# A second block run as one program, with its gated linear unit between two halves of the attention branch

## The reference, cut to what matters

```
attn = sliding_window_attention(q, k, v, sinks)                  # 256 x 1024
y_val, y_gate = split(gelu(s5_ssm(u)) @ w_glu + b_glu)           # 512 -> 2 x 512
ssm = y_val * sigmoid(y_gate)                                    # 256 x 512
merged = sigmoid(gate_attn) * (attn @ w_branch_attn)             # 1024 -> 2048
       + sigmoid(gate_ssm) * (ssm @ w_branch_ssm)                # 512 -> 2048
x = x + merged @ w_out
h = rms_norm(x)
val, gate = split(h @ w_up)                                      # 2048 -> 2 x 5632
x = x + (val * gelu(causal_conv(gate))) @ w_down
out = rms_norm(x)
```

## Time and profile before

| | us |
|---|---|
| median of 3 runs | 3060.67 (3060.24 to 3062.17) |
| the profiled execution's own time | 3060.64 |
| span of its trace | 3058.8 |
| PE busy in it | 2850.6 (93%) |
| PE weight loads | 2793.8 (91%) |
| DVE busy | 1841.8 (60%) |
| ACT busy | 1234.2 (40%) |
| POOL busy | 513.3 (17%) |
| granted PE clock, mean | 0.968 of full |

### The profile page before, as it was taken

One profiled execution on the slowest core, in us unless ns is written; L12 is line 12 of the kernel. 1 busy time (PEld: TensorE's weight loads), 2 busy tenths in 40 slices (PEclk: granted clock), 3 DMA queues, 4 the chain that ended last, 5 costly groups with the idle time before them and its releaser, 6 DMA issues. The chain is left out here.

```text
span 3058.8 us, 60793 instructions
## 1 busy us (share of the span) xinstructions
PE 2850.6 (93%) x24170; PEld 2793.8 (91%) x24170; DVE 1841.8 (60%) x2106; ACT 1234.2 (40%) x1472; POOL 513.3 (17%) x586
## 2 busy tenths in 40 slices
PE   7998687799998999999999969999889999999997
PEld 7998585689997999999999969999889999999997
DVE  7657744556443565554555566698556655765665
ACT  4344112353332544343434434533345443444343
POOL 1000120337000325810191120000121010010011
PEclk9999788899999999999999989999999999999999
DMA  6553000354651656575656635555455565565554
GB/s 228 193 193 108 14 1 1 138 177 153 210 190 55 209 188 194 195 235 193 192 193 193 234 110 184 203 173 173 142 169 184 200 193 193 192 196 194 192 190 145
DMA packets 138262, 513.89 MB, mean 168 GB/s; under 512 B 15344, under 2 KB 15600, under 8 KB 136816
## 3 DMA queue, kind: packets, MB, share of 16 engines
q1 hardware_dynamic: 138096, 511.58, 50.7%
HBM read 503.12 MB, written 8.40 MB: 167 GB/s over the span
## 5 line engine op out<-in xcount | busy, mean ns | idle before, releaser
L638 PE MATMUL acc<-a,hi 128*128 128x256 f32 x3136 | 873.4, 279 | 41.3 <-DVE lo L465 30.8
L639 PE MATMUL acc<-a,hi 128*128 128x256 f32 x3136 | 868.2, 277 | 0.0
L640 PE MATMUL acc<-a,lo 128*128 128x256 f32 x3136 | 868.1, 277 | 0.0
L465 DVE TENSOR_TENSOR lo<-raw,hi 128x1024 fp32r<-128x1024 f32 x416 | 524.9, 1281 | 368.9 <-ACT hi L351 367.4
L638 PE MATMUL acc<-a,hi_f 128*128 128x256 f32 x2304 | 637.5, 277 | 11.7 <-DVE lo_f L465 11.0
L639 PE MATMUL acc<-a,hi_f 128*128 128x256 f32 x2304 | 637.1, 277 | 0.0
L640 PE MATMUL acc<-a,lo_f 128*128 128x256 f32 x2304 | 637.0, 276 | 0.0
L638 PEld LDWEIGHTS acc<-a,hi 128*128 128x128 f32 x3136 | 590.9, 188 | 46.1 <-issue 37.1
L639 PEld LDWEIGHTS acc<-a,hi 128*128 128x128 f32 x3136 | 591.0, 188 | 0.8 <-issue 0.5
L640 PEld LDWEIGHTS acc<-a,lo 128*128 128x128 f32 x3136 | 590.9, 188 | 0.0
L465 DVE TENSOR_TENSOR lo_f<-raw_f,hi_f 128x1024 fp32r<-128x1024 f32 x288 | 383.3, 1343 | 334.1 <-ACT hi_f L351 333.6
(11 more groups left out here) (509 smaller groups left out, 4277.7 us busy)
## 6 DMA issues: line engine op xcount, KB each, us to landing
raw_f<-in_ffn SPq DMA_DIRECT2D x256, 512.0 KB, 3.6
raw_in<-in_w_in SPq DMA_DIRECT2D x96, 512.0 KB, 3.5
raw<-in_w_in SPq DMA_DIRECT2D x92, 512.0 KB, 3.7
raw<-in_up_gate SPq DMA_DIRECT2D x88, 512.0 KB, 4.2
raw<-in_up_val SPq DMA_DIRECT2D x88, 512.0 KB, 4.3
raw<-in_down SPq DMA_DIRECT2D x88, 512.0 KB, 3.4
raw_x<-in_w_out SPq DMA_DIRECT2D x32, 512.0 KB, 4.2
raw_x<-in_wq SPq DMA_DIRECT2D x32, 512.0 KB, 3.3
```

What stands on the lines that cost most here:

```text
L465: eng.tensor_tensor(self.lo[:, slot, :], self.raw[:, slot, :], self.hi[:, slot, :].bitcast(F32), ALU.subtract).then_inc(self.s_lo, 1)
L638: eng.matmul(out, self.hi[:, slot, cols], a[:, 0, :], start=opens, stop=False)
L639: eng.matmul(out, self.hi[:, slot, cols], a[:, 1, :], start=False, stop=False)
L640: ins = eng.matmul(out, self.lo[:, slot, cols], a[:, 0, :], start=False, stop=closes)
```

## The change

- The two programs become one: the lists of phases are joined, the barriers and the clearing between them are gone, and so are `prefetch`, `ahead`, `split` and `skip`. The semaphores are allocated in the outer scope and given back in one list at the end of the feed-forward, ahead of the final norm.
- `br_attn` is cut in two halves of 4 units. The order becomes `br_attn` (first half), `glu_g`, `glu_v`, `br_attn` (second half), `br_ssm`, `w_out_2`.
- `glu_v` writes its result to tiles 4 to 7 of `a0`, no longer to `ah`, which the second half of `br_attn` still reads. `br_ssm` reads it there and writes to `a1`; `w_out_2` reads `a1` and writes `a0`; the `gate` and `val` phases read `a0`, `val` writes `a1` and `down` reads it. Before, these had `a0` and `a1` the other way round. `a1` keeps its place in memory, over the tables.
- `br_ssm` gets `lead`: in its unit v ACT makes the copy of chunk v+1 (in unit 0 those of chunks 0 and 1) ahead of the finish of unit v-1. Its loop is written out (`body` 8).

```diff
@@ def act
-                if not (ph is split and isinstance(v, int) and v == 0):
+                if ph.lead:
+                    for w in range(0 if v == 0 else v + 1, min(v + 2, ph.units)):
+                        self.act_split(eng, ph, w, w)
+                else:
                     self.act_split(eng, ph, v, j, first if first and v == 0 else None,
                                    first if first and v == 1 else None)
...
-        if ahead:
-            self.act_split(eng, ahead, 0, 0)
@@ def dve
-                for k in range(0 if ph is split and isinstance(v, int) and v == 0 else ph.nc):
+                for k in range(ph.nc):
...
-        for k in range(ahead.nc if ahead else 0):
-            self.split_low(eng, ahead, 0, 0, k)
@@ def second_block, into which gates_and_branches goes
+        sem = semaphores(nc, st)
+        with ExitStack() as early:
+            tab = alloc(nc, early, "s_tab", [P, 2, S5_COLS])
+            reals = alloc(nc, early, "s_xr", [P, 2, QT, T])
+            small = [alloc(nc, early, n, [P, 2, NH]) for n in ("mxs", "nmx", "smw", "skw")]
+            slp = alloc(nc, early, "slp", [P, NH])
         room = alloc(nc, st, "a1_room", [P, (LINE - 128) // 4])
         a1 = alloc(nc, st, "a1_3", [P, KT, 2, T], F32R)
...
-        ba = s.phase("br_attn", "br_attn", 8, 2, 2, ah, "br_attn", out=ub,
+        ba = s.phase("br_attn", "br_attn", 4, 2, 2, ah, "br_attn", out=ub,
                      ready=lambda eng: eng.wait_ge(window.low, 4))
         g1 = s.phase("glu_g", "glu", 2, 1, 4, s.a0, "glu_gate", out=gl, g="b_glu", g0=4,
                      ready=lambda eng: eng.wait_ge(space.low, 1))
-        g2 = s.phase("glu_v", "glu", 2, 1, 4, s.a0, "glu_val", out=ah, src=gl, w0=2)
-        bs = s.phase("br_ssm", "br_ssm", 8, 1, 4, ah, "br_ssm", out=s.a0, src=ub, g0=KT, after=g2)
-        phs = [ba, g1, g2, bs]
-        wo = s.phase("w_out_2", "w_out_2", 8, 4, 2, s.a0, "resid", g="ffn2_g", after=bs)
+        g2 = s.phase("glu_v", "glu", 2, 1, 4, s.a0, "glu_val", out=s.a0, t0=4, src=gl, w0=2)
+        bb = s.phase("br_attn", "br_attn", 4, 2, 2, ah, "br_attn", out=ub, t0=8, w0=8)
+        bs = s.phase("br_ssm", "br_ssm", 8, 1, 8, s.a0[:, 4:8], "br_ssm", out=a1, src=ub, g0=KT, after=g2, lead=True)
+        wo = s.phase("w_out_2", "w_out_2", 8, 4, 2, a1, "resid", out=s.a0, g="ffn2_g", after=bs)
+        phs = [ba, g1, g2, bb, bs, wo]
...
-                s.prefetch(eng, wo)
...
-                s.act(eng, phs, aside=space.act_last, at=ba, last=ps, ahead=wo)
+                s.act(eng, phs, aside=space.act_last, at=ba, last=ps)
...
-                s.dve(eng, phs, aside=space.dve_last, at=ba, last=ps, ahead=wo)
+                s.dve(eng, phs, aside=space.dve_last, at=ba, last=ps)
```

More of the change, by code:

```diff
@@ L140 @@
     ready: object = None
+    lead: bool = False
     base: object = None
@@ L308, in prefetch, with act @@
             self.load(eng, ph, c, c)
-    def act(self, eng, phs, aside=None, emit=None, at=None, last=None, ahead=None, split=None):
+    def act(self, eng, phs, aside=None, emit=None, at=None, last=None):
         at = at or phs[-1]
@@ L432, in act_finish, with dve @@
             ins.then_inc(done, 1)
-    def dve(self, eng, phs, aside=None, at=None, emit=None, last=None, finish=True, ahead=None, split=None):
+    def dve(self, eng, phs, aside=None, at=None, emit=None, last=None, finish=True):
         at = at or phs[-1]
@@ L1896, with __init__ @@
     BANKS = 4
-    def __init__(self, nc, s, ua, ah, pa, tab, keys, probs, stack):
+    def __init__(self, s, ua, ah, pa, tab, keys, probs, small, slp, sem):
         self.s, self.ua, self.ah, self.pa = s, ua, ah, pa
@@ L1904, in __init__ @@
         self.pt = probs.rearrange("p (a b) t -> p a (b t)", a=2)
-        self.mxs, self.nmx, self.sm, self.sk = (alloc(nc, stack, n, [P, 2, NH]) for n in ("mxs", "nmx", "smw", "skw"))
-        self.slp = alloc(nc, stack, "slp", [P, NH])
-        sem = semaphores(nc, stack)
+        self.mxs, self.nmx, self.sm, self.sk = small
+        self.slp = slp
         (self.zeroed, self.slopes, self.placed, self.vturned, self.vcopied, self.scored, self.biased, self.maxed,
@@ L2165, with __init__ @@
     EACH = 9
-    def __init__(self, nc, dram, s, ua, pa, gates, window, states, tab, xr, xi, bq, stack):
+    def __init__(self, dram, s, ua, pa, gates, window, states, tab, xr, xi, bq, sem):
         self.dram, self.s, self.ua, self.pa, self.gates, self.window = dram, s, ua, pa, gates, window
@@ L2355, in second_block @@
         clear_pads(nc, s)
-        wo = gates_and_branches(nc, dram, s, ub, ah, ua, states)
+        sem = semaphores(nc, st)
[4 more added lines that the diff above has]
+            slp = alloc(nc, early, "slp", [P, NH])
         room = alloc(nc, st, "a1_room", [P, (LINE - 128) // 4])
         a1 = alloc(nc, st, "a1_3", [P, KT, 2, T], F32R)
[L2359 to L2398, removed]
         xr = reals[:, 0], reals[:, 1]
@@ L2401, in gates_and_branches @@
         bq = ua[:, Q2 + QT:Q2 + 2 * QT, :].rearrange("p a t -> p (a t)"), s.th[:].rearrange("p a b t -> p (a b t)")
+        gl = ua[:, Q2:Q2 + 4, :]
         spare = ub[:, 0:2, :]
@@ L2409, in gates_and_branches @@
                      g0=GA2 + 2 * raw, w0=w0 + 4 * raw)
-        window = WindowAttention(nc, s, ua, ah, pa, tab, xr[0], ub[:, KT:2 * KT, :], st)
-        space = StateSpace(nc, dram, s, ua, pa, ps, window, states, tab, xr, xi, bq, st)
-        ba = s.phase("br_attn", "br_attn", 8, 2, 2, ah, "br_attn", out=ub,
+        window = WindowAttention(s, ua, ah, pa, tab, xr[0], ub[:, KT:2 * KT, :], small, slp, sem)
+        space = StateSpace(dram, s, ua, pa, ps, window, states, tab, xr, xi, bq, sem)
+        ba = s.phase("br_attn", "br_attn", 4, 2, 2, ah, "br_attn", out=ub,
                      ready=lambda eng: eng.wait_ge(window.low, 4))
@@ L2415, in gates_and_branches @@
                      ready=lambda eng: eng.wait_ge(space.low, 1))
-        g2 = s.phase("glu_v", "glu", 2, 1, 4, s.a0, "glu_val", out=ah, src=gl, w0=2)
-        bs = s.phase("br_ssm", "br_ssm", 8, 1, 4, ah, "br_ssm", out=s.a0, src=ub, g0=KT, after=g2)
-        phs = [ba, g1, g2, bs]
-        wo = s.phase("w_out_2", "w_out_2", 8, 4, 2, s.a0, "resid", g="ffn2_g", after=bs)
+        g2 = s.phase("glu_v", "glu", 2, 1, 4, s.a0, "glu_val", out=s.a0, t0=4, src=gl, w0=2)
[3 more added lines that the diff above has]
+        phs = [ba, g1, g2, bb, bs, wo]
+        for q, t0 in enumerate((0, KT, 2 * KT)):
+            n = min(KT, FT2 - t0)
+            gate = s.phase("gate", "up_gate", n // 2, 4, 2, s.a0, "gate", out=ub, g="c2", g0=3 * t0, p0=t0,
+                           taps=3, w0=2 * t0, after=wo if q == 0 else None, sum_after=q == 0)
+            val = s.phase("val", "up_val", n // 2, 4, 2, s.a0, "val", out=a1, src=ub, w0=2 * t0)
+            down = s.phase("down", "down", 8, n // 4, 4 if n % 16 else 2, a1, "sumsq" if q == 2 else "acc",
+                           w0=32 * q, after=val)
+            phs += [gate, val, down]
         with nc.Block() as block:
@@ L2480, in _ @@
                 s.pe(eng, phs)
-    return wo
+    final_norm(nc, s, "final2_g", out_dram)
 def build(nc, dram, out_dram):
```

## The result

The changed kernel takes 3038.9 us (median of 4 runs, 3032.3 to 3043.1), the one before 3061.4 in the same session (3060.2 to 3063.3): the ratio is 0.9924, with a 95% interval of 0.9911 to 0.9936. In a later session it was 3037.8 against 3062.1, ratio 0.9922 (0.9905 to 0.9938). So some 23 us are gone, 0.77%.

The account below looks back on a forecast made before the run. PE bounds the kernel, losing 32.3 us from glu_g to w_out_2's second chunk. With 8.1 lost after, 24.2 won less 0.8 for clearing gives 23.4 off 3060.64: 3037.2 us, range 3033.5 to 3041.

Parts of the forecast that it names:

- GLU after four units: glu_g starts 21.8 us earlier at no cost, its input being ready; the GLU's own losses of 1.48 + 1.03 stay.
- Second half of `br_attn`: Behind glu_v: the 3.99 us wait for POOL goes, 1.2 lost waiting for DVE's first subtraction; clock stays full.
- `br_ssm` with the lead: ACT's copy leaves the circle in br_ssm; 2.0 us lost there, bounds 0.3 to 3.5.
- the circle through DVE and POOL: In br_ssm, POOL waits for DVE's subtraction and L517 for POOL: 3.06 us a chunk.
- its chunks 2 to 7 start 2.9 to 3.1 apart: Sign to look for in PE's timeline of br_ssm: a pitch of 2.9 to 3.1 us.
- Rival (a): POOL and DVE don't meet: br_ssm loses 1.0 us, the step to w_out_2 1.8; 3035.6 us; chance 0.20.
- Step into `w_out_2`: From br_ssm: the lead ends, ACT copies w_out_2's first chunk behind unit 6's finish; 2.4 us lost, bounds 0.5 to 3.5.
- Clearing: Giving back the semaphores between feed-forward and final norm costs 0.8 us more, bounds 0.3 to 1.6.
- Swap of the buffers: a0 and a1 trade places in w_out_2 and feed-forward; matmuls take 0.1132 us from either, so 0 cost.
- Rival (b): PE's clock falls in br_attn's second half after three idle gaps; price 2.5 to 2.8 us, 3040 us; chance 0.08.
- (c): In br_ssm the lead frees nothing because ACT's early copy waits; pitch near 4.4, 12 us lost, 3047 us; chance 0.05.
- (d): Buffer swap slows w_out_2 and feed-forward, some 298 chunks; 0.1 us more each gives 3067 us; chance 0.02.

Follow-up runs that it names:

- two_ahead: lead_all, but in br_ssm ACT copies two chunks ahead of its finish and DVE subtracts one ahead of its evacuation; 3031.6 us, ratio 0.9899.
- lead_over: Changed kernel with ACT's lead carried over the phase border: w_out_2's first chunk copied ahead of the finish of br_ssm's unit 6; 3035.8 us, ratio 0.9920.
- no_clear: Changed kernel with the second block's semaphores held to the program's end, so no clearing ahead of the final norm; 3041.0 us, ratio 0.9937.
- lead_all: lead_over with the lead also in glu_g and glu_v and into the second half of br_attn; 3030.4 us, ratio 0.9904.
- both: Changed kernel with the edits of lead_all and no_clear together; 3031.8 us, ratio 0.9903.

## Why the prediction was right

The forecast was 3037.2, and two medians of the changed kernel are 3038.9 and 3037.8. Some of that nearness is luck: the four runs behind the first median reach from 3032.3 to 3043.1, beyond the forecast range on both sides, and the first block alone can move a run by more than most of the terms. By its own steps, in the profiled execution:

- *GLU after four units.* 0 was forecast for `glu_g`'s wait, and PE does not wait there. 1.48 + 1.03 was kept, and measured 1.48 + 1.03.
- *Second half of `br_attn`.* 1.2 was forecast, 1.20 at the gap and 0.11 in the next chunk were measured. The clock held there: the first chunk behind the gap took 2.80 to 2.83 in all executions with these three gaps.
- *`br_ssm` with the lead.* The term that was mis-sized: 2.0 was forecast, 0.9 measured. For the circle through DVE and POOL the prediction took "1.14 + 1.30 + 0.62 = 3.06 a chunk". In `two_ahead`, where DVE from 2196.36 on no longer waits for PE, this circle is 2.84. Of the 0.22 too much, 0.07 lies between the subtraction's start and POOL's end (2200.45 - 2198.08 = 2.37 for 2.44), and the rest behind POOL's end, where the next subtraction starts 0.46 and not 0.62 later. So the circle through PE, which stood beside it with 2.8 to 2.94, is the longer one, at 2.87; in the changed kernel L515 waits for PE, and POOL has all but ended when L517 comes. The sign "its chunks 2 to 7 start 2.9 to 3.1 apart" was met by three of the six steps only: they are 2.83 to 2.91. Rival (a), with 1.0 for `br_ssm`, had this number right but not its reason: POOL and DVE do meet, and it costs PE next to nothing there.
- *Step into `w_out_2`.* 2.4 forecast, 2.06 and 0.08 measured, and the fourth chunk did not wait. It was "ACT's finish and copy", as `lead_over` shows; PE's idle there was 1.78.
- *Clearing.* 0.8 forecast; 0.62 measured for itself, but with the clock it came to 1.4 in one execution and 0.7 in the other. The prediction had no term for the clock there.
- *Swap of the buffers.* 0 forecast, and 1767 matmuls per 200 us on both sides.

Lost: 6.9 for 8.1. Won there 25.4 for 24.2, less 1.5 at the end for 0.8, together 23.9 where 23.4 was forecast. The three errors, 1.1 and 0.3 in favour and 0.7 against, cancel in part. Rival (b), a fall of the clock, came true in one of the three profiled executions that have the 2.0 us step (the changed kernel's two and `no_clear`), but behind that step and not in `br_attn`, and at 1.6 us, not 2.5 to 2.8; where (b) had put it, the clock held. (c) and (d) are refuted by the pitch and by the feed-forward.

## What to carry to other kernels

Where an engine does the next chunk's work behind the finish of the last, and the next engine does the same, follow the circle and add up its links; if the slowest engine is no link of it, one instruction moved ahead frees that engine. Let the engines lead by different distances, the upstream one further, or the circle closes again one chunk on (4.45 with equal leads, 2.72 with two and one). And ask what a test would show if the rival were true: over eight chunks a lead hides any pitch that is only a little too slow. Where a result's last unit must pass three engines before the next phase, put independent work in between, and look at what the phase's first chunk truly needs: the border between the programs cost 10.7 us, because all had to finish ahead of anything of the next.

## What the runs showed of the hardware

An idle stretch of PE of 1.8 us did not decide on the clock: behind the same one the granted clock was 1.00 in one execution and 0.62 in another, which took 1.6 us more for one chunk. The same at the final norm, where behind one idle of 3.7 us four matmuls took from 1.10 to 2.05.

A POOL and a DVE instruction, both with two inputs in SBUF, take turns to within about a tenth of a microsecond in these rows. Begun 0.8 us into DVE's subtraction, POOL's took 1.54 for 1.28, and the subtraction its 1.22; where DVE's L538 came while POOL was at work, it took 1.07 for 0.69. A waiting instruction so looks stretched, not late. The turns close up by tenths: DVE's pitch was 2.84 where lone durations, put one behind the other, had added up to 3.06. By the rule of the Trainium skill that the prediction weighed (SBUF — State Buffer, section "SBUF: two separate sides"), one holds the port until it is done; the rows agree in that the one that came later is the one that grew, and in roughly how much: the subtraction ended at 2199.29, POOL's at 2200.45, 1.16 later, and L538 0.55 after that, at 2201.00, against 1.28 and 0.69 alone.

The first block's mixers swing by 8 us over the profiled executions, with the same code. Medians over 4 runs could not order `lead_all`, `two_ahead` and `both`; the time between two landmarks in the trace, repeatable to 0.1 us but for the clock (85.99 and 85.96, 80.60 and 80.63, 79.55 and 79.55 for pairs of kernels with this part alike), could.
